# Differential attention on one core: weights formed in one pass, work moved between engines, and extra transposes of the identity at each head's boundary

## What is computed

```
q, k = rope(rms_norm(q, q_g)), rope(rms_norm(k, k_g))      # 8 heads x 2 halves c x 64
s    = einsum(q, k) * 64 ** -0.5, masked block-causally by chunks of 64
p    = softmax(s)                                           # for each half c
a    = p[c=0] - lam * p[c=1]
o    = rms_norm(a @ v, sub_g) * (1 - lambda_init)           # v is 128 wide
```

## Time and profile before

| | us |
|---|---|
| median of 3 runs (lowest, highest) | 2373.98 (2370.65, 2377.41) |
| the profiled execution: its own time | 2388.6 |
| its span, from first to last instruction | 2387.0 |
| heads 0 to 6 with the projection of the next one (from the first to the eighth turn of q and k) | 229.6 |
| the last head and the step to the next stage | 31.7 |
| everything behind it | 2070.4 |

### The profile page before, as it was taken

How to read it: one execution, slowest core, us unless ns; L and a number is a source line. 1 busy time by engine, 2 the same in 40 slices (tenths; PEclk the granted TensorE clock), 3 DMA queues, 4 the chain that set the end, 5 groups by cost and what they waited for, 6 DMA issues and landing times. The chain is left out here.

```text
span 2387.0 us, 30282 instructions
## 1 busy us (share of the span) xinstructions
PE 2257.5 (95%) x10196; PEld 1809.4 (76%) x10196; DVE 1591.8 (67%) x1790; ACT 1300.9 (55%) x1526; POOL 293.5 (12%) x391
## 2 busy tenths in 40 slices
PE   5888889799999999999989999999999999999997
PEld 4777777566566688888768888888888888888885
DVE  4676744454333433434569889888889888889884
ACT  5444444233322343323337777777777777777773
POOL 1232210200122100000010110110110110110110
PEclk8998999999899999999879999999999999999998
DMA  4111033211111234334469999999999999999992
GB/s 174 36 44 53 14 128 99 102 62 53 36 36 36 90 96 132 132 97 121 196 236 353 371 365 376 358 364 369 358 369 369 367 363 368 364 365 373 362 366 88
DMA packets 89012, 515.72 MB, mean 216 GB/s; under 512 B 15108, under 2 KB 16132, under 8 KB 38184
## 3 DMA queue, kind: packets, MB, share of 16 engines
q1 hardware_dynamic: 79736, 498.14, 56.2%
q0 software_dynamic: 9216, 16.81, 2.9%
HBM read 508.59 MB, written 23.33 MB: 223 GB/s over the span
## 5 line engine op out<-in xcount | busy, mean ns | idle before, releaser
L1991 DVE TENSOR_TENSOR moe_lo<-moe_raw,moe_hi 128x2048 fp32r<-128x2048 f32 x382 | 855.0, 2285 | 17.5 <-ACT moe_hi L1984 14.4
L1984 ACT ACTIVATE moe_hi<-moe_raw 128x2048 fp32r<-128x2048 f32 x380 | 728.4, 1919 | 166.6 <-PE bank L2002 159.5
L2000 PE MATMUL bank<-moe_hi,moe_XTh 128*128 128x512 f32 x1024 | 403.7, 394 | 0.0
L2001 PE MATMUL bank<-moe_lo,moe_XTh 128*128 128x512 f32 x1024 | 403.6, 394 | 0.0
L2002 PE MATMUL bank<-moe_hi,moe_XTl 128*128 128x512 f32 x1024 | 403.3, 394 | 0.0
L166 ACT ACTIVATE unit_hi<-unit_raw 128x1024 fp32r<-128x1024 f32 x116 | 122.4, 1059 | 261.9 <-DMA unit_raw<-in_w_units 241.7
L172 DVE TENSOR_TENSOR unit_lo<-unit_raw,unit_hi 128x1024 fp32r<-128x1024 f32 x116 | 143.2, 1238 | 177.4 <-ACT unit_hi L166 174.8
L2002 PEld LDWEIGHTS bank<-moe_hi,moe_XTl 128*128 128x128 f32 x1024 | 193.1, 189 | 44.4
L2001 PEld LDWEIGHTS bank<-moe_lo,moe_XTh 128*128 128x128 f32 x1024 | 193.1, 189 | 44.3
L2000 PEld LDWEIGHTS bank<-moe_hi,moe_XTh 128*128 128x128 f32 x1024 | 193.7, 189 | 40.3
L2000 PE MATMUL bank<-moe_hi,moe_aTh 128*128 128x512 f32 x512 | 200.6, 392 | 1.4 <-DVE moe_aTl L2112 1.4
(11 more groups left out here) (349 smaller groups left out, 3687.0 us busy)
## 6 DMA issues: line engine op xcount, KB each, us to landing
moe_raw<-in_w_moe SPq DMA_DIRECT2D x384, 1024.0 KB, 7.0
unit_raw<-in_w_units SPq DMA_DIRECT2D x116, 512.0 KB, 3.6
da_slab<-in_w_qkv SPq DMA_DIRECT2D x8, 1536.0 KB, 6.5
x_sb<-in_x SPq DMA_DIRECT2D x4, 512.0 KB, 5.1
yda_d<-y_daT SPq DMA_DIRECT2D x1, 2048.0 KB, 6.2
y_daT<-in_blocks_qk SPq DMA_DIRECT2D x1, 2048.0 KB, 8.0
y_daT<-yda_d SPq DMA_DIRECT2D x1, 2048.0 KB, 8.1
y_daT<-in_x SPq DMA_DIRECT2D x1, 2048.0 KB, 9.7
```

What stands on the lines that cost most here:

```text
L1984: nc.scalar.activation(HI[ring(n, pos)][:], RAW[pos][:], ACT.Copy).then_inc(s_hi, 1)
L1991: nc.vector.tensor_tensor(LO[pos][:], RAW[pos][:], HI[ring(n, pos)][:].bitcast(F32), ALU.subtract).then_inc(s_lo, 1)
L2000: nc.tensor.matmul(bank[:], xh[:, x], HI[ring][:, w], start=start and k == 0, stop=False)
L2001: nc.tensor.matmul(bank[:], xh[:, x], LO[pos][:, w], start=False, stop=False)
```

## The change

Six edits, all in `stage_da` but the first:

1. The banks are allocated in pairs, so that one DVE instruction can read two of them. `negmax` does one memset and one maximum over both halves c, after both pairs of score matmuls.
2. The weights `a` are left unnormalised: `ratio = lambda * l0 / l1`, then one pass `a = E1 * ratio + E0`. ACT multiplies the output by `1 / l0` (the scale of `keep_o`'s square and copy).
3. The last multiplication of the rotated q and k (block 3) goes from POOL to DVE; POOL only makes the reciprocal root and signals it (`s_rs`). DVE signals `s_last`.
4. `turn_qk` is split by block: the six transposes of blocks 0 to 2 go ahead of `pv(h, 3)`, the two of block 3 stay behind it.
5. `spin(n)` transposes the identity n times into bank 0, which nothing reads afterwards: 5 ahead of `pv(h, 3)`, 3 behind it, 8 ahead of `scores(h+1, 0)`, 7 behind it. It waits for nothing but that ACT has read the third projection out of bank 0.
6. The copy to `y_daT` goes from DVE to ACT, behind `exps(h+1, 0)`.

```
@@ -97,7 +97,8 @@
...
         self.base = {}
-        self.banks = [ctx.enter_context(nc.psum_tensor(f"bank{i}", [P, 512], F32)) for i in range(8)]
+        self.pairs = [ctx.enter_context(nc.psum_tensor(f"bank{2 * i}", [P, 2, 512], F32)) for i in range(4)]
+        self.banks = [self.pairs[i // 2][:, i % 2, :] for i in range(8)]
         self.cols = self.sb("cols", [P, NCOL])
...
@@ -283,15 +284,16 @@
...
     a, aT = sb("a", [P, S]), sb("aT", [P, S])
-    mx, rl = sb("mx", [P, 2]), sb("rl", [P, 2])
+    mx, rl, ratio = sb("mx", [P, 2]), sb("rl", [P, TT, 2]), sb("ratio", [P, 1])
     nm, l = ([sb(n + str(i), [P, 2]) for i in range(2)] for n in ("nm", "l"))
     osq, oss, ors, on = sb("osq", [P, P]), sb("oss", [P, TT]), sb("ors", [P, TT]), sb("on", [P, TT, P])
+    sub = sb("sub", [P, 1])
     pj, aTb, ob, qkb = K.banks[0:2], K.banks[4], K.banks[5], K.banks[6:8]
-    Sb = [K.banks[2:4], qkb]
+    Sb, Sp = [K.banks[2:4], qkb], [K.pairs[1], K.pairs[3]]
     (s_proj, s_pjA, s_pjD, s_ss, s_rope, s_qkT, s_qkTe, s_S, s_nm, s_exp, s_a, s_aT, s_aTe, s_pv, s_oss,
-     s_ors, s_on, s_yT, s_yTe, s_wh, s_wl, s_onr, s_kTe, s_ku) = (K.sem("da_" + n) for n in (
+     s_ors, s_on, s_yT, s_yTe, s_wh, s_wl, s_onr, s_kTe, s_ku, s_rs, s_last) = (K.sem("da_" + n) for n in (
          "proj", "proj_used_act", "proj_used_dve", "sumsq", "rotated", "qkT", "qT_kept", "scores",
-         "negmax", "exp", "a", "aT", "aT_kept", "pv", "o_sumsq", "o_rstd", "o_kept", "yT", "yT_kept", "slab_hi", "slab_lo", "o_scaled", "kT_kept", "ca_unit_used"))
+         "negmax", "exp", "a", "aT", "aT_kept", "pv", "o_sumsq", "o_rstd", "o_kept", "yT", "yT_kept", "slab_hi", "slab_lo", "o_scaled", "kT_kept", "ca_unit_used", "last_rstd", "last_rotated"))
     projs = {0: [0], 1: [1], 2: [2, 3], 3: []}
...
@@ -355,14 +357,17 @@
...
-            def turn_qk(n, first=False):
-                pe.wait_ge(s_rope, n * 4 + 4)
+            def turn_qk(n, i, first=False):
+                if i < TT - 1:
+                    pe.wait_ge(s_rope, n * 3 + (i + 1))
+                else:
+                    pe.wait_ge(s_last, n + 1)
                 if not first:
...
                 for c in range(2):
-                    for i in range(TT):
-                        mm = nc.tensor.transpose(qkb[c][:, i * P:(i + 1) * P], qk[:, i, c * P:(c + 1) * P], K.ident[:])
-                mm.then_inc(s_qkT, 1)
+                    mm = nc.tensor.transpose(qkb[c][:, i * P:(i + 1) * P], qk[:, i, c * P:(c + 1) * P], K.ident[:])
+                if i == TT - 1:
+                    mm.then_inc(s_qkT, 1)
...
@@ -381,6 +386,11 @@
...
                 mm.then_inc(s_pv, 1)
+
+            def spin(n):
+
+                for _ in range(n):
+                    nc.tensor.transpose(pj[0][:, 0:P], K.ident[:], K.ident[:])
...
@@ -405,10 +415,18 @@
...
                         ca_keys(3, i - 2)
+                if more:
+                    for i in range(TT - 1):
+                        turn_qk(h + 1, i)
+                    pe.wait_ge(s_pjA, (h + 1) * 4 + 3)
+                    spin(5)
                 pv(h, par, TT - 1)
                 if more:
-                    turn_qk(h + 1)
+                    spin(3)
+                    turn_qk(h + 1, TT - 1)
+                    spin(8)
                     scores(h + 1, 1 - par, 0)
+                    spin(7)
                 pe.wait_ge(s_onr, h + 1)
...
@@ -416,7 +434,8 @@
...
                 proj(0, 0, i, True)
-            turn_qk(0, True)
+            for i in range(TT):
+                turn_qk(0, i, True)
             scores(0, 0, 0)
...
@@ -438,9 +457,15 @@
...
                     act.wait_ge(s_yT, START + h)
-                nc.scalar.activation(osq[:], ob[:, i * P:(i + 1) * P], ACT.Square,
+                nc.scalar.activation(osq[:], ob[:, i * P:(i + 1) * P], ACT.Square, scale=rl[:, i, 0:1],
                                      accum_out=oss[:, i:i + 1]).then_inc(s_oss, 1)
-                nc.scalar.activation(on[:, i, :], ob[:, i * P:(i + 1) * P], ACT.Copy).then_inc(s_on, 1)
+                nc.scalar.activation(on[:, i, :], ob[:, i * P:(i + 1) * P], ACT.Copy,
+                                     scale=rl[:, i, 0:1]).then_inc(s_on, 1)
+
+            def keep_y(h):
+                act.wait_ge(s_yT, START + h + 1)
+                y = K.y_daT[:, h * S:(h + 1) * S] if isinstance(h, int) else K.y_daT[:, ds(h * S, S)]
+                nc.scalar.activation(y, aTb, ACT.Copy, scale=sub[:]).then_inc(s_yTe, 1)
...
@@ -481,6 +506,7 @@
...
                     exps(h + 1, 0)
+                keep_y(h)
...
@@ -502,7 +528,11 @@
...
                 hold(K, pool, s_ss, n * 4 + (i + 1))
-                chain(rstd(pool, nc, chain, rs[:, i, :], ss[:, i, :], DH, K.half[:, 0:4]))
+                op = rstd(pool, nc, chain, rs[:, i, :], ss[:, i, :], DH, K.half[:, 0:4])
+                if i == TT - 1:
+                    op.then_inc(s_rs, 1)
+                    return
+                chain(op)
                 hold(K, pool, s_pjD, n * 4 + (i + 1))
...
@@ -536,7 +566,7 @@
...
                                         ALU.add).then_inc(s_ss, 1)
-                dve.wait_ge(s_rope, n * 4 + i)
+                dve.wait_ge(s_rope, n * 3 + i)
                 src = raw[:].rearrange("p (g c d) -> p g c d", g=2, c=2)
...
@@ -546,18 +576,22 @@
...
                                               Sn[:, :, 32:64].unsqueeze(2).broadcast_to([P, 2, 2, 32]), ALU.mult))
-                nc.vector.tensor_tensor(t1[:], t1[:], t2[:], ALU.add).then_inc(s_pjD, 1)
+                op = nc.vector.tensor_tensor(t1[:], t1[:], t2[:], ALU.add).then_inc(s_pjD, 1)
+                if i == TT - 1:
+                    dve.wait_ge(s_pjD, n * 4 + 4)
+                    dve.wait_ge(s_rs, n + 1)
+                    dve.wait_ge(s_qkT, n)
+                    nc.vector.tensor_tensor(qk[:, i, :].rearrange("p (g d) -> p g d", g=4),
+                                            t1[:].rearrange("p (g d) -> p g d", g=4),
+                                            rs[:, i, :].unsqueeze(2).broadcast_to([P, 4, DH]), ALU.mult).then_inc(s_last, 1)
             def negmax(h, i, wait=True):
-                n, banks = (i + 1) * P, Sb[i % 2]
+                n, pair = (i + 1) * P, Sp[i % 2]
                 if wait:
                     dve.wait_ge(s_nm, h * 4 + i)
-                for c in range(2):
-                    dve.wait_ge(s_S, h * 8 + (2 * i + c + 1))
-
-                    chain(nc.vector.memset(banks[c][0:64, n - 64:n], NEG))
-                    op = nc.vector.tensor_reduce(mx[:, c:c + 1], banks[c][:, 0:n], AX, ALU.max)
-                chain(op)
+                dve.wait_ge(s_S, h * 8 + (2 * i + 2))
+                chain(nc.vector.memset(pair[0:64, :, n - 64:n], NEG))
+                chain(nc.vector.tensor_reduce(mx[:], pair[:, :, 0:n], AX, ALU.max))
                 nc.vector.tensor_scalar(nm[i % 2][:], mx[:], -scale, None, ALU.mult).then_inc(s_nm, 1)
...
@@ -576,11 +610,11 @@
...
                     dve.wait_ge(s_a, START + h * 4 + i)
-                    chain(nc.vector.reciprocal(rl[:], l[e][:]))
-                    chain(nc.vector.tensor_tensor(rl[:, 1:2], rl[:, 1:2], K.lamv[:, 4:5], ALU.mult))
+                    chain(nc.vector.reciprocal(rl[:, i, :], l[e][:]))
+                    chain(nc.vector.scalar_tensor_tensor(ratio[:], rl[:, i, 1:2], K.lamv[:, 4:5], l[e][:, 0:1], ALU.mult,
+                                                         ALU.mult))
                     dve.wait_ge(s_aT, START + h * 4 + i)
-                    chain(nc.vector.tensor_scalar(a[:, 0:n], E[e][1][:, 0:n], rl[:, 1:2], None, ALU.mult))
-                    nc.vector.scalar_tensor_tensor(a[:, 0:n], E[e][0][:, 0:n], rl[:, 0:1], a[:, 0:n], ALU.mult,
+                    nc.vector.scalar_tensor_tensor(a[:, 0:n], E[e][1][:, 0:n], ratio[:], E[e][0][:, 0:n], ALU.mult,
                                                    ALU.add).then_inc(s_a, 1)
...
@@ -598,10 +632,6 @@
...
                     negmax(h + 1, 0)
-                dve.wait_ge(s_yT, START + h + 1)
-                y = K.y_daT[:, h * S:(h + 1) * S] if isinstance(h, int) else K.y_daT[:, ds(h * S, S)]
-                nc.vector.tensor_scalar(y, aTb[:], K.col("g_sub"), 1.0 - LAMBDA_INIT, ALU.mult,
-                                        ALU.mult).then_inc(s_yTe, 1)
...
@@ -609,6 +639,7 @@
...
             chain(nc.vector.tensor_scalar(K.lamv[:, 4:5], K.lamv[:, 4:5], -LAMBDA_INIT, None, ALU.add))
+            chain(nc.vector.tensor_scalar(sub[:], K.col("g_sub"), 1.0 - LAMBDA_INIT, None, ALU.mult))
             for i in range(TT):
...
```

## The result

The changed kernel took 2360.1 us, median of 4 runs (2359.4 to 2362.5), beside 2374.4 us for 4 runs of before. The ratio is 0.9942, 95% interval 0.9925 to 0.9960: faster by 14.3 us, half of the 28.1 us forecast. The time lies 5 us above the forecast's own range of 2338 to 2355, and inside the wider 2337 to 2362 that also covers two rivals.

The account below looks back on a forecast made before the run. Low TensorE clock at head boundaries and waits between engines were taken as the bound; 14.8 + 3.9 + 0.2 + 7.3 + 1.5 + 0.4 = 28.1 us off 2374.0 gives 2346, range 2338 to 2355, wider 2337 to 2362.

Parts of the forecast that it names:

- two rivals: Clock only half won (2353, reaching to 2361, chance 0.16); DVE shortened but not the head (2359, chance 0.03).
- the clock's term: Boundaries behind the first head: spins and earlier work hold TensorE's clock, 14.8 us gained, bounds 0 and 17.5.
- the chain's: Shorter waits between engines: six boundaries 3.9 us, eighth turn 0.2 us, inside the heads 7.3 us.
- What bounds the kernel: Heads 0 to 6 of stage_da: 229.63 us against 212.1 at full clock, 17.5 us from the lower clock; also waits between engines.
- the clock is only half won: Rival: a boundary can still fall, or unprofiled runs had fewer low stretches; half of 14.8 us lost, 2353, chance 0.16.
- The rival at 2359 us: DVE gets shorter but the head does not, ACT's chain being as long; 13.3 us fall away, chance 0.03.
- Boundary: From T(3) to yT between heads: yT at 5.8 us instead of 6.45, 0.65 us at each of six, 3.9 us.
- the prediction's sign: Expected in the changed profile: 7.1 us from T(3) to the projection, 7.80 in the good boundary before.
- the eighth turn: Boundary that did not wait for POOL: 0.2 us gained.
- Inside the heads: Cheaper negmax and one-pass weights remove TensorE's waits for `a` in heads 0 to 6: 7.3 of 7.7 us, bounds 4 and 7.7.
- First turn and last head: First turn earlier by 1.5 us, between 0 and 2.5; in the last head T(3)'s wait for `a` shortened by 0.4 us.
- That the spins hold the clock: Identity transposes in boundary waits count as work for TensorE's clock; rival that they do not: 2370, chance 0.08.

Follow-up runs that it names:

- the matched pair: Second profile of the unedited kernel before, and the profile of the unedited changed kernel run again; their spans differ by 19.3 us.
- the second profile of before: The kernel before, unchanged, profiled once more: heads 0 to 6 took 221.3 us at clock 0.94; median of 10 runs 2379.3 us.

## Why the prediction was right and wrong

All comparisons together: before 2379.0 us, mean of 71 runs; the changed kernel 2361.6, mean of 16. The change gives about **17 us, 0.7%**; each comparison by itself gave 14.3, 19.3 and 14.7. The direction and the mechanism were right. The size was not: of the 10.7 us between 28.1 and 17.4 about 6 are the clock's term and 3 the chain's; the rest is less than the comparisons differ by.

*What bounds the kernel, and the clock term: the step that failed.* I wrote that 17.5 us is the lower clock and took 14.8 of it for the gain. The reading of the profile was right: seven heads at full clock take 212 us. But the number of boundaries at which the clock falls changes from execution to execution of the same program; the next profile showed 221.3 us, 9.3 us over 212 instead of 17.5. In the matched pair the heads gained 17.1 us. At full clock a head of after is 1.2 us shorter (29.0 against 30.2), 8.5 us in seven; so the clock's part is **about 8.6 us instead of 14.8**. That is an estimate from one pair of profiles, but the runs agree with it roughly: their mean clocks give 153 us at 1.2 GHz before and 127 after, 25 us less, which at 0.40 us each is 10 us. And I had the warning in hand: the profiled execution stood 14.6 us above the median, and I wrote that nothing showed this difference to lie in the edited stage. It was the same clock, in good part in that stage. A term read from the slowest execution was subtracted from the median. The rival "the clock is only half won" had this in its second half, fewer low stretches to win in the runs, and 0.16 of the chance; its first half, boundaries that fall in spite of the spins, did not happen. The rival at 2359 us, where the chain gains nothing, came within 1 us of the measured 2360.1 by luck: the chain gained 8.5 us.

*Boundary.* 0.48 us each instead of 0.65; 7.3 us from T(3) to the projection, where the prediction's sign was 7.1. The spins and the ACT wait were placed within 0.1 us. Mis-sized was what ACT's scale costs. I took 0.07 us from copies of 1024 columns; it is 0.09 (0.27 to 0.36), three times on the path to yT, and I let it count for `pv` alone. Without the scales yT stands at 5.81 (forecast 5.8), with them at 5.97. At the eighth turn, where I had 0.2 us gained, yT follows T(3) by 6.05 us instead of 5.85: 0.2 lost. The Trainium skill has the scale's price ("ScalarE: Activation LUTs", What ACT_TABLE_LOAD costs: a pointer operand adds about 93 ns to an ACTIVATE); the trace agrees.

*Inside the heads.* The waits went as said, but T(1) still follows 0.13 us late: 0.8 us a head, against 1.04. The paired maximum is as priced (two maxima of 384 columns were 1.12 us, one over both banks is 0.96); the memset over two banks takes 0.17 us instead of 0.11. Boundary and inside together gained 8.5 us, forecast 11.4. Inside the heads 5.9 of the 7.3 us came, between the bounds of 4 and 7.7.

*First turn and last head.* From the last projection of head 0 to the next one it was 8.63 us in the second profile of before and is 6.94 in the changed kernel: 1.7 against 1.5. But where before's clock fell later there (7.76 us with spins alone), only 0.8 is left. T(3) of the last head waits 2.3 us instead of 2.7, 0.4 as forecast.

*That the spins hold the clock* was right, and for the reason given: transposes count. With spins the clock fell at no boundary between heads in any of seven profiles; without them it fell at three or more in each of five, at 25 of 35 in all. By the rule of the Trainium skill that the prediction weighed ("TensorE: Matmul & The Clock Gate", Part 4, PE-mode transpose), the spins could not have done this; the traces do not agree with it. And at the boundaries where before's clock fell TensorE had no idle gap above 1.2 us. At 217.9, ahead of the turn of the earlier trace rows, the gaps are those of the earlier trace rows, where it stayed:

```profile
216.16 1.13 PE L381 MATMUL bank<-da_v,da_aT 128*128 128x128 f32 x8 [1.20 <-ACT da_on L443]
```

*What stays open.* The first comparison's 4 runs of before have a median of 2374.4 us, 4 to 5 us under those of three other comparisons; whether that is the chip or chance wasn't separated. Which part of the 17 us the boundary edits bring once the spins are there wasn't tried.

## What to carry to other kernels

Where a kernel's stalls let TensorE's clock fall, one profile is one draw: compare the profiled time with the spread of the runs before reading a term from it, and look at the mean clock of each run. Transposes of the identity into a free bank, as many as the wait holds (0.12 us each), kept the clock at no cost that these runs show. They were worth 4 us in the kernel before and 8 to 12 in the changed one. Price a shorter stall together with its clock: the shorter boundary alone gained nothing, while the shorter work inside the heads gained 8.5 us by itself. And read a head between marks that stand alike at both ends. Look for such waits in every stage; the untouched mLSTM stage gave some us more.

## What was not expected of the hardware

The time behind the edited stage is not constant for constant instructions. In the eleven profiles with the same instructions there it took 2063.4 to 2076.9 us, and with it the time at 1.2 GHz in it went from 97 to 124 us: close to half a us for each us. So a gain in one stage can be given back or doubled in another by where the later stalls fall. No run tells whether an edit can steer that.

At the boundary POOL's multiplication for block 3 and DVE's slab_lo slow each other. The multiplication took 0.61 us where it began first or had no slab_lo beside it, and 1.23 to 1.42 behind it; slab_lo took 0.96 us, and 1.40 where it began second. So the 1.24 us that the prediction took for POOL's pace are this collision's, and edit 3 ends it: DVE's multiplication takes 0.42 us, and slab_lo behind it 0.95.
